# Reordering VectorE's and ScalarE's work in the Gated DeltaNet heads of a two-block model

## What is computed

```python
proj = xn @ w_in                                    # q, k, v, z of every head, and the gates
qkv = silu(causal_dwconv(proj[..., :3072], conv_w))  # four taps
q, k, v = l2norm(q) * 128 ** -0.5, l2norm(k), v
beta, g = sigmoid(b_raw), -exp(A_log) * softplus(a_raw + dt_bias)
# per head and chunk, gcum = cumsum(g):
m = strict(beta * k @ k.T * exp(gcum_i - gcum_j))
u, w = triangular_solve(m + eye, [v * beta, k * beta * exp(gcum)])
v_new = u - w @ state
o = (q * exp(gcum)) @ state + (q @ k.T * decay) @ v_new
state = state * exp(gcum[-1]) + (k * exp(gcum[-1] - gcum)).T @ v_new
out = (rmsnorm(o) * silu(z)) @ w_out
```

## Time and profile before

| | |
|---|---|
| median of three runs | 1824.33 us |
| the profiled execution | 1826.3 us |
| its span, first to last instruction | 1824.6 us |
| mean granted clock of TensorE | 0.994 of full |
| the eight heads | from about 53 to 369 us of the span |
| distance of two steady heads | 40.6 us |

### The profile page before, as it was taken

How to read it: one execution, slowest core, us unless ns; L and a number is a source line. 1 busy time by engine, 2 the same in 40 slices (tenths; PEclk the granted TensorE clock), 3 DMA queues, 4 the chain that set the end, 5 groups by cost and what they waited for, 6 DMA issues and landing times.

```text
span 1824.6 us, 23727 instructions
## 1 busy us (share of the span) xinstructions
PE 1776.0 (97%) x8122; PEld 1406.7 (77%) x8122; DVE 1189.3 (65%) x1948; ACT 843.4 (46%) x1360; POOL 35.8 (2%) x65
## 2 busy tenths in 40 slices
PE   9999999889999999999998999999999999999997
PEld 6777777667888888888886788888888776777885
DVE  6888888656777753367776577777433588765444
ACT  5554454344444432257777444444322455643222
POOL 1000000000000000000000000000001000000000
PEclk9999999999999999999999999999999999999999
DMA  5522212022222232133332232221421312222321
GB/s 185 171 68 62 68 57 63 31 81 93 92 92 92 80 127 95 66 118 108 105 96 72 94 102 92 92 92 61 155 95 51 104 36 69 87 80 92 103 92 58
DMA packets 44826, 163.27 MB, mean 89 GB/s; under 512 B 5874, under 2 KB 6149, under 8 KB 44769
## 3 DMA queue, kind: packets, MB, share of 16 engines
q1 hardware_dynamic: 39872, 148.00, 24.3%
q0 software_dynamic: 4464, 14.47, 2.8%
q10 hardware_dynamic: 432, 0.07, 0.0%
HBM read 155.89 MB, written 6.63 MB: 89 GB/s over the span
## 4 chain that ended last, share of the span: by engine, by line
PE 90%; DVE 6%; ACT 3%; issue 1%; DMA 0%; SPq 0%; DVEq 0%; ACTq 0%
PE acc L584 23%; PE acc L585 23%; PE acc L586 23%; PE acc L610 7%; DVE wsplit L1655 1%; PE pb L727 1%; PE pc L744 1%; PE pd L1015 1%; PE pa L1003 1%; ACT wsplit L1138 1%; PE pa L705 1%; PE pd L954 1%; PE pd L953 1%; PE pa L585 1%; PE pa L584 1%
## 5 line engine op out<-in xcount | busy, mean ns | idle before, releaser
L584 PE MATMUL acc<-xhi,wsplit 128*128 128x512 f32 x1200 | 496.9, 414 | 1.1 <-DVE at_vs L2075 1.0
L1138 ACT ACTIVATE wsplit<-wraw 128x1024 fp32r<-128x1024 f32 (+1 forms) x252 | 276.3, 1097 | 462.5 <-PE acc L586 426.4
L585 PE MATMUL acc<-xlo,wsplit 128*128 128x512 f32 x1200 | 475.8, 396 | 0.0
L586 PE MATMUL acc<-xhi,wsplit 128*128 128x512 f32 x1200 | 475.5, 396 | 0.0
L1655 DVE TENSOR_TENSOR wsplit<-wraw,wsplit 128x1024 fp32r<-128x1024 f32 (+1 forms) x250 | 318.1, 1273 | 147.8 <-ACT wsplit L1138 146.8
L584 PEld LDWEIGHTS acc<-xhi,wsplit 128*128 128x128 f32 x1200 | 226.2, 189 | 60.3 <-issue 5.3
L585 PEld LDWEIGHTS acc<-xlo,wsplit 128*128 128x128 f32 x1200 | 226.5, 189 | 55.4 <-issue 4.3
L586 PEld LDWEIGHTS acc<-xhi,wsplit 128*128 128x128 f32 x1200 | 226.0, 188 | 54.8
L610 PE MATMUL acc<-xhi,wsplit 128*128 128x512 f32 x464 | 159.0, 412 | 5.7 <-DVE wsplit L1655 5.7
L586 PE MATMUL acc<-hid_hi,wsplit 128*128 128x512 f32 x352 | 139.6, 396 | 0.0
L585 PE MATMUL acc<-hid_lo,wsplit 128*128 128x512 f32 x352 | 139.5, 396 | 0.0
(11 more groups left out here) (379 smaller groups left out, 2616.2 us busy)
## 6 DMA issues: line engine op xcount, KB each, us to landing
wraw<-w SPq DMA_DIRECT2D x220, 512.0 KB, 3.3
wraw<-w SPq DMA_DIRECT2D x32, 704.0 KB, 4.1
bias_dram<-ext_dram POOLq DMA_DIRECT2D x1, 4096.0 KB, 20.8
bias<-bias_dram POOLq DMA_DIRECT2D x16, 256.0 KB, 3.0
at_ks<-at_ks SPq DMA_DIRECT2D x16, 256.0 KB, 2.9
crow<-row_dram POOLq DMA_DIRECT2D x8, 256.0 KB, 3.7
brow<-row_dram POOLq DMA_DIRECT2D x8, 256.0 KB, 4.5
outT<-h SPq DMA_DIRECT2D x8, 256.0 KB, 2.2
```

Source lines behind the costliest of these rows:

```text
L584: mm(out, whi[:, k, :], a[:, x_at + k, :], start=(k == first), stop=False)
L585: mm(out, whi[:, k, :], b[:, x_at + k, :], start=False, stop=False)
L586: m = mm(out, wlo[:, k, :], a[:, x_at + k, :], start=False, stop=(k == last))
L1138: A(split(s, j, 0), raw(s, j), ACT.Copy).then_inc(w_hi_ready, 1)
```

## The change

Only orders and counts change; every operation is still there, and the arithmetic is the same. On TensorE one piece moves from behind the fourth x product to behind the third join product, one output piece of the last head moves, and two pieces of tile (i + 1, 0) move ahead of the recurrence. On ScalarE the cast of tile (i, 3) goes behind the newest tap of q. On VectorE the low part of tile (i, 3) moves from behind `solve` into gap 1, the taps of q and k move back, the low part of tile (i + 1, 0) moves ahead of the copy into `tt`, and the decayed q and the low part of the outputs go behind `solve`. In the opening the masks are built ahead of the gates' chain, and the low part of tile (0, 2) comes ahead of the first `gram`. The special first body of VectorE's loop goes.

```diff
@@ the counts of pieces (TensorE)
-            AFTER_SOLVE, AFTER_X, AFTER_JOIN = 14, [5, 5, 4, 4], [5, 5, 3, 3]
-            OUT_SOLVE, OUT_X, OUT_JOIN = (0, 5), [(5, 6), (6, 7), (8, 9), (10, 10)], [(6, 6), (7, 8), (9, 10), (10, 11)]
-            BEFORE_STATE, AFTER_KS, AFTER_V, AFTER_S = 2, [0, 2, 3, 3], [3, 0, 3, 3], [3, 3, 3, 0]
+            AFTER_SOLVE, AFTER_X, AFTER_JOIN = 14, [5, 5, 4, 3], [5, 5, 4, 3]
+            OUT_SOLVE, OUT_X, OUT_JOIN = (0, 4), [(4, 5), (6, 7), (8, 9), (10, 10)], [(5, 6), (7, 8), (9, 10), (10, 11)]
+            BEFORE_STATE, AFTER_KS, AFTER_V, AFTER_S = 4, [0, 2, 3, 3], [3, 0, 3, 3], [3, 3, 3, 0]
@@ delta(i) (ScalarE)
                 if not last:
+                    conv_newest(1, i + 1, i)
                     cast_ahead(s, i, 1, False)
-                    conv_newest(1, i + 1, i)
@@ the opening (VectorE): the masks move up, ahead of the gates
             conv_older(-1, 1, 0, (1,))
+            block8 = cst[:, C_BLOCK, :]
+            tt_(block8, cst[:, C_LOW, :], cst[:, C_LOW + 1, :], ALU.add).then_inc(ev("solve_dve"), 1)
...
+            nc.vector.memset(yx[:, :, 0:1], 1.0).then_inc(ev("solve_dve"), 1)
             dve.wait_ge(ev("gate_act"), at(GATE_ACT, "gate_ln"))
...
             take(-1, 3)
-            block8 = cst[:, C_BLOCK, :]
-            tt_(block8, cst[:, C_LOW, :], cst[:, C_LOW + 1, :], ALU.add).then_inc(ev("solve_dve"), 1)
...
-            nc.vector.memset(yx[:, :, 0:1], 1.0).then_inc(ev("solve_dve"), 1)
             conv_older(-1, 3, 0)
@@ between(gap) in delta(i) (VectorE)
                     if last:
                         if gap == 0:
-                            decayed_q(i)
-                            low_of_outputs(i - 1)
-                        if gap == 1:
                             low_after(o, 0, 2)
                         return
                     if gap == 0:
                         take(i, 1)
-                        decayed_q(i)
                     if gap == 1:
-                        conv_older(i, 1, i + 1, (1,))
+                        low(s, i, 3)
                     if gap == 2:
-                        conv_older(i, 1, i + 1, (2, 3))
+                        conv_older(i, 1, i + 1, (1, 2))
                     if gap == 3:
+                        conv_older(i, 1, i + 1, (3,))
                         take(i, 2)
-                    if gap in (4, 5, 6):
-                        conv_older(i, 2, i + 1, (gap - 3,))
+                    if gap == 4:
+                        conv_older(i, 2, i + 1, (1,))
+                    if gap == 5:
+                        conv_older(i, 2, i + 1, (2,))
+                    if gap == 6:
+                        conv_older(i, 2, i + 1, (3,))
+                        low(s, i + 1, 0)
                     if gap == 7:
-                        low(s, i + 1, 0)
                         take(i, 3)
@@ the end of delta(i) (VectorE)
                     unit_qk(i + 1)
-                    if not (isinstance(i, int) and i == 0):
-                        low_of_outputs(i - 1)
                     with_q(i)
...
                     solve(i + 1)
-                    if not last_qkv:
-                        low(s, i + 1, 3)
+                    decayed_q(i + 1)
+                    low_of_outputs(i)
@@ ahead of the first head (VectorE)
             take(0, 0)
+            low(s, 0, 2)
             gram(0)
-            low(s, 0, 2)
             solve(0)
-            low(s, 0, 3)
-            delta(0, False)
-            with dve.Fori(1, HA - 2) as i:
+            decayed_q(0)
+            with dve.Fori(0, HA - 2) as i:
                 delta(i, False)
```

More of the change, by code:

```diff
@@ L1739, in _ @@
             conv_older(-1, 1, 0, (1,))
+            block8 = cst[:, C_BLOCK, :]
+            tt_(block8, cst[:, C_LOW, :], cst[:, C_LOW + 1, :], ALU.add).then_inc(ev("solve_dve"), 1)
+            dve.wait_ge(ev("solve_dve"), 1)
+            tt_(block8, block8, cst[:, C_LOW + 2, :], ALU.add).then_inc(ev("solve_dve"), 1)
+            dve.wait_ge(ev("solve_dve"), 2)
+            nc.vector.transpose(xm[:, 0, :], block8).then_inc(ev("solve_dve"), 1)
+            dve.wait_ge(ev("solve_dve"), 3)
+            tt_(block8, ident, block8, ALU.subtract).then_inc(ev("solve_dve"), 1)
+            dve.wait_ge(ev("solve_dve"), 4)
+            tt_(block8, block8, xm[:, 0, :], ALU.subtract).then_inc(ev("solve_dve"), 1)
+            ts_(cst[:, C_MIN, :], cst[:, C_INCL2 + 1, :], 1.0, -NEG, ALU.subtract, ALU.mult).then_inc(ev("solve_dve"), 1)
+            nc.vector.tensor_reduce(e8[:], ident.rearrange("p (b c) -> p c b", c=B), AX_X, ALU.add).then_inc(ev("solve_dve"), 1)
+            dve.wait_ge(ev("solve_dve"), 7)
+            ts_(en[:], e8[:], -1.0, None, ALU.mult).then_inc(ev("solve_dve"), 1)
+            nc.vector.memset(yx[:, :, 0:1], 1.0).then_inc(ev("solve_dve"), 1)
             dve.wait_ge(ev("gate_act"), at(GATE_ACT, "gate_ln"))
```

## The result

The changed kernel takes 1839.3 us (median of 4 runs, 1838.38 to 1840.94), the kernel before, run beside it, 1825.32 us (1822.76 to 1826.86). The ratio is 1.008, with a 95% interval of 1.0065 to 1.0093: slower by 14 us, where 13.0 had been predicted (1837.3, range 1829 to 1843). The total is close, but the prediction's account of the pieces ahead of the state, of what a head hangs on and of the last head does not hold as it stands, and the errors partly cancel.

A forecast was written before the change was run, and what follows sets the result against it. The prediction took TensorE as the bound (97% of the span). Seven heads x 1.33 = 9.3, the opening 4.2 and the last head -0.5 gave 13.0 us on 1824.3: 1837.3, range 1829 to 1843.

The forecast's parts named there:

- part 5: Opening: masks ahead of gates' chain and low part of tile 2 ahead of Gram multiply; first solve product 4.2 us late.
- Part 3: Solve of each head: tile 3's low part in gap 1 makes TensorE wait 0.89; second add at +8.29 instead of +7.48.
- Part 4: Gaps 3 to 6 of each head: moved tap and longer wait delay the next z tile; loss 1.33 per head.
- The term of -0.5: Gaps 3 to 6: the low part ahead of the copy saves 0.35 of work and 0.15 of wait.
- Part 1: Two pieces moved from behind the state to before it: plus 0.47, minus 0.47, a head comes out even.
- Part 2: Behind the first turned block: decayed q and outputs' low part replace tile 3's low part; nothing won, nothing lost.
- Part 6: Last head: output weights' low part moves from gap 1 to gap 0; 0.5 won, moved output piece costs nothing.
- A: Rival, faster: low parts are in time at tile 3 and in the opening; -4.0 us, 1820.3; chance 0.06.
- B: Rival, no change: heads come out even, opening and last head add 1.7 to 3.7; 1826.0 to 1828.0; chance 0.11.
- D: Rival, slower by less: heads lose 0.3 to 0.8 each, opening as worked out; 1830 to 1833.5; chance 0.15.
- C: Rival, slower still: the opening's two stalls pull down TensorE's clock, 1 to 3 more; 1838.5 to 1840.5; chance 0.20.

The follow-up runs named there:

- after, two pieces: Changed kernel with two pieces instead of four ahead of the state: 1843.1 us, ratio 1.0098.
- after, tile 3 in gap 0: Changed kernel with tile 3's cast ahead of the newest tap again and its low part in gap 0: 1835.68 us, ratio 1.006.
- after, tap back: Changed kernel with the third tap of q moved back from gap 3 into gap 2: 1835.71 us, ratio 1.0057.
- both: Changed kernel with tile 3's cast ahead, its low part in gap 0, and the third tap of q back in gap 2: 1833.8 us, ratio 1.0046.
- both, and a tap in gap 1, the last run of the taps: Changed kernel with tile 3's cast ahead, its low part in gap 0, q's third tap in gap 2, first tap in gap 1: 1827.11 us, ratio 1.0004.
- before, z in gap 6: Kernel before with the low part of the z tile moved from gap 7 to gap 6, ahead of the copy into tt: 1825.08 us, ratio 0.9995.
- before, z in gap 6, four pieces: Kernel before with the z tile's low part in gap 6 and four pieces instead of two ahead of the state: 1820.32 us, ratio 0.9973.
- before, four pieces: Kernel before with four pieces instead of two ahead of the state, nothing else: 1825.37 us, ratio 0.9997.
- the run that casts first: Changed kernel with tile 3's cast ahead of the newest tap of q again, its low part left in gap 1: 1841.05 us, ratio 1.0086.
- five output pieces: Changed kernel with five output pieces of the last head ahead of its first solve product again: 1838.93 us, ratio 1.0079.
- the run with the masks alone: Kernel before with the opening's masks moved ahead of the gates' chain, nothing else: 1828.14 us, ratio 1.0016.
- the run with the low part alone: Kernel before with the opening's low part of tile 2 ahead of the Gram product's mask multiply, nothing else: 1827.52 us, ratio 1.0013.

## Why the total came out close, and which steps did not hold

**The opening (part 5) stands.** 4.2 was predicted, 4.07 came. On TensorE, against the earlier trace rows:

```profile
30.73 0.41 PE L659 MATMUL pb<-gg,cst 128*128 128x32 f32 x2 [2.04 <-DVE gg L1759]
...
56.13 0.70 PE L711 MATMUL pa<-xm,cst 128*128 128x256 f32 x2 [2.19 <-DVE xm L1811]
...
61.08 1.16 PE L727 MATMUL pb<-tn,gd 128*128 128x128 f32 x8 [0.98 <-DVE tn L1839]
```

And VectorE's low part of tile 2, which waits for its cast while the Gram product's multiply stands behind it:

```profile
51.43 1.23 DVE L1655 TENSOR_TENSOR wsplit<-wraw,wsplit 128x1024 fp32r<-128x1024 f32 x1 [3.79 <-ACT wsplit L1138]
```

Counted from the norm product (1.47 earlier in this trace), the first x product stands at what would be 62.55; 62.6 was written.

**Part 3, the late tile 3, stands as an event.** The first piece of tile 3 was to start at +5.92 and did at +5.93; the second join product at +7.2, measured +7.18; the second add at +8.29, measured +8.27. By starts that first piece is 0.90 later than before (0.89 written); the bracket shows 0.66 because it counts from the modelled end of the matmul ahead.

**Part 4 measured its 1.33 at the z tile alone.** The waits inside it came out: 0.72 ahead of the tap of k (0.75 written), and the z tile starts at +17.28 (+17.4 written), 1.22 later than before. But in the kernel before the head does not hang on that piece. Line 797 starts there 0.05 after the end of `vn`, and `vn` hangs on the take of v, through ScalarE's newest tap. The take moved by more, 17.40 - 15.85 = 1.55: 1.21 with the start of the low part (+14.72 to +15.93), and 0.34 because the copy into `tt`, which stood ahead of the low part, now stands between it and the take. The term of -0.5 ("the low part goes ahead of the copy") holds for the z tile; for the take of v the copy's 0.35 of work is not saved.

**Part 1 is the step that failed.** It said: "Ahead of the state the same two pieces cost 0.47, so a head comes out even". The runs with two and four pieces show otherwise: four win 0.47 in the changed kernel, 0.46 with the low part of z in gap 6, and 0.19 on the kernel before. Ahead of the state they fill time in which TensorE would wait for `vn`. The gain itself needed no new mechanism: the prediction had it, and cancelled it against a cost that it had not looked up in the trace. The lines of `vn`, 0.8 to 1.8 us behind the take of v, show that it is not there; the prediction read past them. The misses of parts 1 and 4 cancel in part: without the two pieces the change costs 1.55 a head (42.15 - 40.6) where 1.33 was written, and the pieces win 0.47 where nothing was written.

What the runs give in place of parts 1 and 4 is one sum. From the first x product of a head to the next it is the start of the take of v, plus about 1.8 to line 797 (1.76 with two pieces, 1.83 with four), plus 23.0 with two pieces ahead of the state or 22.45 with four. The column "z tile" is the start of its first piece:

| kernel | second add | z tile | take of v | line 797 | pieces | head, worked out | measured |
|---|---|---|---|---|---|---|---|
| before | 7.48 | 16.06 | 15.85 | 17.61 | 2 | 40.65 | 40.6 |
| after | 8.27 | 17.28 | 17.40 | 19.23 | 4 | 41.65 | 41.68 |
| after, two pieces | 8.28 | 17.29 | 17.41 | 19.16 | 2 | 42.21 | 42.15 |
| after, tile 3 in gap 0 | 7.64 | 16.64 | 16.76 | 18.59 | 4 | 41.01 | 41.04 |
| after, tap back | 8.80 | 16.81 | 16.93 | 18.77 | 4 | 41.18 | 41.2 |
| both | 8.55 | 16.56 | 16.68 | 18.50 | 4 | 40.93 | 40.96 |
| both, and a tap in gap 1 | 7.67 | 15.68 | 15.81 | 17.64 | 4 | 40.06 | 40.08 |
| before, z in gap 6 | 7.49 | 15.50 | 15.63 | 17.38 | 2 | 40.43 | 40.35 |
| before, z in gap 6, four pieces | 7.49 | 15.51 | 15.62 | 17.45 | 4 | 39.87 | 39.89 |
| before, four pieces | 7.49 | 16.06 | 15.86 | 18.01 | 4 | 40.11 | 40.41 |

The constants are read from these rows. Two runs were forecast with them: the one with a tap in gap 1, 0.03 over, and the four pieces alone, for which line 797 was put at +17.94, where the pieces bring it, and the head at 40.4 (measured +18.01 and 40.41). For the change it says +1.55 - 0.48 = +1.07 a head; 1.08 was measured. The prediction's 1.33 a head was 0.25 too much, and its heads 9.3 against 8.7 (heads 0 and 6 lost 1.65 and 1.68). With the low part of z in gap 6 the take of v is 8.1 behind the second add when the third tap stands in gap 2 and 9.1 when it stands in gap 3; so the tap costs 1.0 there, more than its 0.7 of work, since the newest tap of k then comes late as well (a wait of 0.72, and 0.39 with the tap in gap 2).

The last row is 0.30 off, and it shows what the sum leaves out. With two pieces line 797 starts 0.05 after the end of `vn`, in all five profiled kernels that have two. With four it starts 0.12 to 0.21 after it, and 1.94 to 1.96 after the first piece of the z tile, in all nine that have four: there TensorE, going through its pieces, comes last. In the order of the change the take of v starts 0.12 after that first piece, so the two counts differ by 0.07 only (+19.16 for `vn`, +19.23 for the pieces), and the sum by the take holds; in the order of the kernel before the z tile starts 0.2 behind the take, and the pieces decide (16.06 + 1.95 + 22.45 = 40.46, measured 40.41).

**Part 2** was put at nothing. No run isolates it, but the run with a tap in gap 1, which has this part in it, leaves it no more than some hundredths of a us a head.

**Part 6 left out the clock.** Predicted -0.5, measured +0.74 in the profile after. What it worked out is there: from the second x product to the end of the last head it went 0.5 faster, and in the three kernels with four output pieces whose clock held, the whole stretch took 24.05 to 24.07, 0.5 less than before. There the moved piece costs nothing, although the wait ahead of the first x product is 2.33 instead of 1.63. In the profile after the clock fell behind that wait, and the 1.25 of it turn the sign.

**The rivals.** A and B fail by the heads, which lost 8.7 where A wins and B has them even. The Trainium skill (Perfetto Trace Analysis, Identifying the Most-Contended Engine) would have one judge TensorE's room by its flops against the peak and by the weight loads' share, and not by matmul busy time; the share is 77% before and after, and the time grew by 12 us of waits all the same, so it did not tell these cases apart. D fails: the heads lost 1.08. C named a real mechanism: in the profiled run after, the clock held in the opening and fell in the last head, where C did not look, and in other kernels with the same stalls it fell in the opening. The measured median of 1839.3 lies in C's range (1838.5 to 1840.5; 1 to 3 more than 1837.3 would be 0.2 less at each end). So it is partly luck that the forecast's number comes so near: the heads cost 0.6 less than written, the opening 0.1 less, and the clock in the last head 1.25 that no term had.

## What the runs showed of TensorE's clock

The first x product of the last head after, and the windows around it (the third column from the right is the granted clock):

```profile
351.34 2.02 PE L727 MATMUL pb<-tn,gd 128*128 128x128 f32 x8 [2.33 <-DVE tn L1839]
```

```profile
350.00:352.00 2.00, 0.66 (x3) 0.69 (x4) 1.97 (x4) 0.03 (x1) 0.00 (x0) 0.84 0.02 4
352.00:354.00 2.00, 2.00 (x9) 1.82 (x9) 0.97 (x2) 0.00 (x0) 0.00 (x0) 0.50 0.00 0
354.00:356.00 2.00, 2.00 (x13) 1.73 (x11) 1.52 (x3) 0.00 (x0) 0.00 (x0) 0.80 0.00 0
```

After 2.33 idle the clock is 0.50, that is 1.2 GHz, and it comes back to 2.4 GHz in the window 354 to 356; the product takes 2.02 instead of 1.13, and the second x product comes 5.10 behind the first instead of 3.85: the price is 1.25 (1.02 in the run that casts first). The same product before stands behind a shorter idle time:

```profile
340.04 1.13 PE L727 MATMUL pb<-tn,gd 128*128 128x128 f32 x8 [1.63 <-DVE tn L1839]
```

What I had not expected is that it is not certain. The kernel with two pieces ahead of the state has the same idle time and a clock of 1.00:

```profile
355.41 1.13 PE L727 MATMUL pb<-tn,gd 128*128 128x128 f32 x8 [2.33 <-DVE tn L1839]
```

```profile
356.00:358.00 2.00, 1.91 (x14) 1.44 (x14) 1.86 (x3) 0.00 (x0) 0.00 (x0) 1.00 0.00 0
```

Of the seven profiled kernels with the four output pieces and this idle of 2.33, the clock fell in four (the change, tile 3 in gap 0, casting first, the last run of the taps) and held in three. With five pieces, and 1.6 idle, it held in all seven. That makes it likely that the moved piece, by the longer wait, opens the way to the fall; with one execution of each kernel it is not shown. In the opening the stall of 2.04 to 2.06 for the gates was followed by 0.50 in four of the eight profiled kernels that have the whole new opening (casting first, five output pieces, two pieces ahead of the state, the tap back), and not in the run with the masks alone. In these four the opening took 39.9 to 40.7. Behind the second stall, of 2.0 to 2.2 for the spread, the clock fell in four of the eight as well (tile 3 in gap 0, five output pieces, two pieces ahead of the state, the last run of the taps), and not in the run with the low part alone. The two that had only this second fall took 38.8, and the two without either took 38.4. Here is the run with the tap back, where it fell:

```profile
30.00:32.00 2.00, 1.32 (x5) 1.32 (x6) 1.41 (x7) 0.00 (x0) 0.00 (x0) 0.65 0.01 4
32.00:34.00 2.00, 2.00 (x6) 1.50 (x6) 0.84 (x2) 1.74 (x5) 0.00 (x0) 0.50 0.04 8
```

The part behind the heads, in which no edit has anything, scatters too: it took from 1459.97 to 1462.55 us in the 14 profiles. So a profiled span of such a kernel is uncertain by 1 to 4 us (the changed kernel and the one that casts first differ by 4.3, with the same heads), and I compared segments and not spans. Why the clock falls in one execution and not in the next is open. The Trainium skill (Perfetto Trace Analysis, Matmul Optimizations) says that the matmul engine scales power with utilization, so that matmuls should run back to back in batches; the traces agree in kind, with 1.25 us as the price of one such gap, where it was paid.

## What to carry to other kernels

Before a piece of filler work is called a cost, look for what the next dependent instruction waits for, on all engines: in an engine with a strict order that may be an operation standing behind an unrelated one (here a copy behind a convolution's tap), and then the filler is almost free up to that point (0.07 for two pieces here). A head or a loop body is best compared at the instruction that its recurrence hangs on, and not at the first one that is seen to be late. And two reorderings that each show no gain (here 0.9995 and 0.9997) can show one together (0.9973), when each had hidden most of what the other wins: by the heads they won 0.25 and 0.19 us alone and 0.71 together.
